# Gates of a product-key expert layer as fp32r matmuls of 256 columns, stored in contiguous blocks

## What is computed

```python
s1, i1 = lax.top_k(s[:, :, 0], PEER_TOPK)
s2, i2 = lax.top_k(s[:, :, 1], PEER_TOPK)
...
sc, pos = lax.top_k(cand, PEER_TOPK)
eidx = jnp.take_along_axis(cidx, pos, axis=-1)
gate = jax.nn.softmax(sc, axis=-1)
act = jax.nn.gelu(jnp.einsum('thkd,td->thk', e_u[eidx], xt).astype(jnp.float32))
w = (gate * act).astype(xt.dtype)
return jnp.einsum('thk,thkd->td', w, e_v[eidx])
```

## Time and profile before

| what | value |
|---|---|
| median of 3 runs | 4709.73 us (4707.64 to 4710.36) |
| profiled execution, its own time | 4707.14 us |
| its span in the trace | 4705.4 us |
| PE busy | 4426.2 us, 94% of the span |
| DVE / ACT / POOL busy | 2150.1 / 979.1 / 768.2 us |
| mean granted TensorE clock | 0.958 |
| chain that ended last | PE 87%, DMA 7%, DVE 2%, ACT 2% |

### The profile page before, as it was taken

How to read it: one execution, slowest core, us unless ns; L and a number is a source line. 1 busy time by engine, 2 the same in 40 slices (tenths; PEclk the granted TensorE clock), 3 DMA queues, 4 the chain that set the end, 5 groups by cost and what they waited for, 6 DMA issues and landing times.

```text
span 4705.4 us, 56888 instructions
## 1 busy us (share of the span) xinstructions
PE 4426.2 (94%) x23446; PEld 3833.8 (81%) x23446; DVE 2150.1 (46%) x3919; ACT 979.1 (21%) x1607; POOL 768.2 (16%) x532
## 2 busy tenths in 40 slices
PE   6898878879999999999999999979999999999999
PEld 4565546669999999999999999968878788787887
DVE  2222212121397667344444444435555555555554
ACT  1212111121122222222222222211111111111111
POOL 0000000011121222444444444400000000000000
PEclk8988779769999999999999999989999999999999
DMA  4000120011122222244443444464343433434332
GB/s 167 0 0 0 48 125 22 14 38 37 51 92 86 93 93 88 88 128 137 137 127 121 136 137 137 121 221 133 133 135 130 139 131 134 134 131 139 131 134 80
DMA packets 397825, 485.55 MB, mean 103 GB/s; under 512 B 290656, under 2 KB 308584, under 8 KB 396456
## 3 DMA queue, kind: packets, MB, share of 16 engines
q1 hardware_dynamic: 397624, 482.73, 31.2%
HBM read 329.78 MB, written 153.89 MB: 103 GB/s over the span
## 4 chain that ended last, share of the span: by engine, by line
PE 87%; DMA 7%; DVE 2%; ACT 2%; issue 1%; POOL 1%; DVEq 0%; ACTq 0%; SPq 0%; POOLq 0%
PE ps L311 77%; DMA ur<-u_t 5%; PE ps L1000 4%; PE ps L354 1%; PE ps L976 1%; PE ps L814 1%; PE ps L776 1%; DMA win<-w_in 0%; PE ps L305 0%; ACT uh L1045 0%; PE ps L819 0%; DMA gate_in<-gates 0%; DVE xT L552 0%; DMA vc_s<-vc 0%; PE ps L390 0%
## 5 line engine op out<-in xcount | busy, mean ns | idle before, releaser
L311 PE MATMUL ps<-xh,uh 128*128 128x364 f32 (+1 forms) x3456 | 1159.6, 336 | 24.3 <-issue 10.4
L311 PE MATMUL ps<-xh,ul 128*128 128x364 f32 (+1 forms) x3456 | 1140.5, 330 | 8.0 <-issue 8.0
L311 PE MATMUL ps<-xl,uh 128*128 128x364 f32 (+1 forms) x3456 | 1139.7, 330 | 0.0
L311 PE MATMUL ps<-vh,wh 128*128 128x512 f32 (+1 forms) x2304 | 898.2, 390 | 29.3 <-DVE wl L1257 29.3
L311 PE MATMUL ps<-vh,wl 128*128 128x512 f32 (+1 forms) x2304 | 898.1, 390 | 0.0
L311 PE MATMUL ps<-vl,wh 128*128 128x512 f32 (+1 forms) x2304 | 896.9, 389 | 0.0
L1266 DVE TENSOR_TENSOR acc<-acc,ps 128x512 f32<-128x512 f32 (+1 forms) x576 | 394.0, 685 | 710.6 <-PE ps L311 710.6
L311 PEld LDWEIGHTS ps<-xh,uh 128*128 128x128 f32 x3456 | 653.9, 189 | 29.1 <-issue 26.6
L311 PEld LDWEIGHTS ps<-xh,ul 128*128 128x128 f32 x3456 | 653.3, 189 | 10.0 <-issue 10.0
L311 PEld LDWEIGHTS ps<-xl,uh 128*128 128x128 f32 x3456 | 654.3, 189 | 0.0
L1089 POOL TENSOR_TENSOR ul<-ur,uh 128x1024 fp32r<-128x1024 f32 x144 | 362.7, 2519 | 1143.8 <-ACT uh L1045 1143.8
(11 more groups left out here) (210 smaller groups left out, 3567.4 us busy)
## 6 DMA issues: line engine op xcount, KB each, us to landing
hidden_after_gelu<-hid SPq DMA_DIRECT2D x128, 544.0 KB, 3.0
gates<-gs SPq DMA_DIRECT2D x17, 4096.0 KB, 21.1
act_in<-hidden_after_gelu SPq DMA_DIRECT2D x128, 544.0 KB, 5.7
gate_in<-gates SPq DMA_DIRECT2D x128, 544.0 KB, 6.6
ur<-u_t SPq DMA_DIRECT2D x128, 512.0 KB, 4.5
vr<-v_w SPq DMA_DIRECT2D x128, 512.0 KB, 3.5
ur<-wq SPq DMA_DIRECT2D x16, 512.0 KB, 4.1
win<-w_in SPq DMA_DIRECT2D x1, 7168.0 KB, 22.5
```

Of the source, the lines that this page charges most:

```text
L311: i = nc.tensor.matmul(out, lhsT, rhs, start=(k == 0), stop=(k == len(pairs) - 1))
```

## The change

1. Gate matmuls in fp32r. oneA holds plain ones and zeros (fp32r). oneB is `[128, 2, 4, 2, 128]`: for each token two halves side by side, the column one-hot times the high part of the gate (gh) and times the low part (gate minus gh). One matmul of 256 columns per token makes both halves; a quad fills two PSUM banks.
2. DVE makes oneB with 8 `tensor_scalar` per quad (is_equal with a per-partition scalar, times another one), in place of one instruction, and oneA as before. POOL's product is gone; POOL only does `split_low`.
3. ACT copies the high halves (`gates_high`) ahead of the gelu of the same group, and DVE adds the low halves to them (`gates_low`). `c_free` now comes from DVE.
4. PSUM: 4 banks for hidden groups (`h_bank`), 4 for quads. A quad stands behind every 18th matmul of a block, inside the groups.
5. The store of the gates goes out from ACT's queue, as contiguous 32 KB per partition; `gate_in` is now read in 17 pieces of 256 B per partition.
6. PICK = 5: GATE0 = 63, GATE1 = 131, so 13 hidden blocks follow the last gate. The transposes of a tile move behind the next tile's blocks, the last two tiles' come together; then ACT makes gh for all tokens, and DVE its low part.

```diff
-PICK = 6
+PICK = 5
-    gates_d = nc.dram_tensor("gates", [PK, PK, T], F32).ap()
+    gates_d = nc.dram_tensor("gates", [QUADS // HALF, 128, PK, 4 * HALF], F32).ap()
-    oneA = sb("oneA", [128, 4, 4, 128])
-    oneB = sb("oneB", [128, 4, 4, 128])
+    oneA = sb("oneA", [128, 4, 4, 128], F32R)
+    oneB = sb("oneB", [128, 2, 4, 2, 128], F32R)
...
+    def h_bank(g, k):
+
+        return (g * NG + k) % 4
...
-            need(e, "gelu", (g - 2) * NG + k + 1)
+            need(e, "gelu", g * NG + k - 3)
...
+                if quads is not None and (k * len(parts) + m) % 18 == 17:
+                    q = (k * len(parts) + m) // 18
+                    gate_quad(e, quads + q, q)
...
         e.wait_ge(sem("c_oneB"), n + 1)
-        e.wait_ge(sem("c_gated"), n + 1)
...
-            i = nc.tensor.matmul(ps[:, 6 + q % 2, k * 128:(k + 1) * 128], oneA[:, q, k, :], oneB[:, q, k, :],
-                                 start=True, stop=True)
+            i = nc.tensor.matmul(ps[:, 4 + 2 * (q % 2) + k // 2, (k % 2) * 256:(k % 2) * 256 + 256], oneA[:, q, k, :],
+                                 oneB[:, q % 2, k, :, :].rearrange("p a b -> p (a b)"), start=True, stop=True)
...
+        def picking(t, like):
             for j in range(PICK):
...
+            if like >= 1:
+                picks_transposed(e, t - 1, (like - 1) % 2)
...
+                if GATE0 <= g < GATE1:
+                    gates_high(e, (g - GATE0) * 4 + k)
...
+                if k == 0 and GATE0 + 4 <= g <= GATE1 and (g - GATE0) % 4 == 0:
+                    gates_out(e, (g - GATE0) // 4 - 1)
             if g + 2 < NB:
                 split_high(e, g + 2)
+            if GATE0 <= g < GATE1:
+                gates_high(e, (g - GATE0) * 4 + 3)
...
+            if t == NT and j == PICK - 1:
+                picks_kept(e, NT)
+                nc.scalar.activation(gh[:], selT[:, 2, :], ACT.Copy).then_inc(sem("gh_ready"), 1)
...
+        def operands(n):
+            need(e, "c_g", n - 3)
+            nc.vector.tensor_tensor(oneA[:, n % 4, :, :], iota.unsqueeze(1).to_broadcast([128, 4, 128]),
+                                    wide(selT[:, 0, 4 * n:4 * n + 4], 128), ALU.is_equal).then_inc(sem("c_oneA"), 1)
+            need(e, "c_g", n - 1)
+            for k in range(4):
+                tok = slice(4 * n + k, 4 * n + k + 1)
+                nc.vector.tensor_scalar(oneB[:, n % 2, k, 0, :], iota, selT[:, 1, tok], gh[:, tok].bitcast(F32),
+                                        ALU.is_equal, ALU.mult)
+                i = nc.vector.tensor_scalar(oneB[:, n % 2, k, 1, :], iota, selT[:, 1, tok], selT[:, 2, tok],
+                                            ALU.is_equal, ALU.mult)
+            i.then_inc(sem("c_oneB"), 1)
+
+        def gates_low(n):
+            e.wait_ge(sem("c_ghi"), n + 1)
+            nc.vector.tensor_tensor(kept(n), kept(n), quad_gates(n, 1), ALU.add).then_inc(sem("c_free"), 1)
+
+        operands(0)
+        operands(1)
         for n in range(QUADS):
+            gates_low(n)
+            if n + 2 < QUADS:
+                operands(n + 2)
...
-                load(gate_in[:, b % 2, :], gates_d[:, b, :], f"gate_in_{b % 2}")
+                load(gate_in[:, b % 2, :].rearrange("p (h t) -> p h t", t=4 * HALF), gates_d[:, :, b, :].rearrange("h p t -> p h t"), f"gate_in_{b % 2}")
```

More of the change, by code:

```diff
@@ L949, in x_pe, with hidden_block @@
             pe_transposes(xnc[:, n % 2, :], banks(2 * (n % 2), 2), width(n), "c_tx")
-    def hidden_block(e, g, par, after=None):
+    def h_bank(g, k):
+        return (g * NG + k) % 4
+    def hidden_block(e, g, like, quads=None):
+        par = like % 2
         e.wait_ge(sem("u_hi"), g + 1)
@@ L959, in hidden_block @@
         for k, (o, w) in enumerate(TG):
-            need(e, "gelu", (g - 2) * NG + k + 1)
+            need(e, "gelu", g * NG + k - 3)
             parts = [(a[:, par, dc * 128:(dc + 1) * 128], b[:, dc, o:o + w])
                      for dc in range(DC) for a, b in ((uh, xh), (uh, xl), (ul, xh))]
-            mm_sum(ps[:, 3 * par + k, 0:w], parts, "hidden")
-            if after:
-                after(k)
+            for m, (lhsT, rhs) in enumerate(parts):
+                i = nc.tensor.matmul(ps[:, h_bank(like, k), 0:w], lhsT, rhs, start=(m == 0), stop=(m == len(parts) - 1))
+                if m == len(parts) - 1:
+                    i.then_inc(sem("hidden"), 1)
+                if quads is not None and (k * len(parts) + m) % 18 == 17:
+                    q = (k * len(parts) + m) // 18
+                    gate_quad(e, quads + q, q)
     def key_scores(e, c):
@@ L1045, in split_high, with quad_gates, kept, gates_high @@
         nc.scalar.activation(uh[:, g % 2, :], ur[:, g % 2, :], ACT.Copy).then_inc(sem("u_hi"), 1)
-    def gates_kept(e, n):
+    def quad_gates(n, part):
+        return ps[:, 4 + 2 * (n % 2):6 + 2 * (n % 2), :].rearrange("p b (t s j) -> p s j (b t)", t=2, s=2)[:, part, :, :]
+    def kept(n):
+        s = n % HALF * 4
+        return gs[:, n // HALF % 2, :, s:s + 4]
+    def gates_high(e, n):
         hf = n // HALF
@@ L1080, in h_act @@
                 nc.scalar.activation(sel[0:p, t % 2, 2, :], sel[0:p, t % 2, 2, :], ACT.Exp).then_inc(sem("c_exp"), 1)
[L1081 to L1085, removed]
+            if 1 <= t <= NT and j == PICK - 1:
+                picks_kept(e, t - 1)
+            if t == NT and j == PICK - 1:
+                picks_kept(e, NT)
+                nc.scalar.activation(gh[:], selT[:, 2, :], ACT.Copy).then_inc(sem("gh_ready"), 1)
     def split_low(e, g):
@@ L1091, in h_pool @@
     def h_pool(e):
-        def weighted(n):
-            if n % 32 == 0:
-                e.wait_ge(sem("c_selT"), n // 32 + 1)
-            e.wait_ge(sem("c_oneA"), n + 1)
-            nc.gpsimd.tensor_tensor(oneA[:, n % 4, :, :], oneA[:, n % 4, :, :], wide(selT[:, 2, 4 * n:4 * n + 4], 128),
-                                    ALU.mult).then_inc(sem("c_gated"), 1)
-        for g in range(GATE0 + 1):
-            split_low(e, g)
-        for g in range(GATE0, GATE1):
-            n = (g - GATE0) * 4
-            weighted(n)
-            weighted(n + 1)
-            split_low(e, g + 1)
-            weighted(n + 2)
-            weighted(n + 3)
-        for g in range(GATE1 + 1, NB):
+        for g in range(NB):
             split_low(e, g)
@@ L1182, in h_dve @@
         softmaxed(e, ch, NT)
[L1184 to L1192 removed]
+        e.wait_ge(sem("c_selT"), NT + 1)
+        e.wait_ge(sem("gh_ready"), 1)
+        ch(nc.vector.tensor_tensor(selT[:, 2, :], selT[:, 2, :], gh[:].bitcast(F32), ALU.subtract))
+        iota = cst[:, C_IOTA:C_IOTA + 128]
+        def operands(n):
[3 more added lines that the diff above has]
+            need(e, "c_g", n - 1)
+            for k in range(4):
+                tok = slice(4 * n + k, 4 * n + k + 1)
[9 more added lines that the diff above has]
+        operands(1)
+        for n in range(QUADS):
+            gates_low(n)
+            if n + 2 < QUADS:
+                operands(n + 2)
     def output_quad(e, qd, par):
```

77 lines of the change are left out of this document (31 added, 46 removed).

## The result

| | before | after |
|---|---|---|
| median | 4708.68 us (4705.12 to 4710.36, 4 runs) | 4799.85 us (4798.37 to 4805.55, 4 runs) |
| profiled execution, span | 4707.14, 4705.4 | 4798.37, 4796.6 |
| granted clock | 0.958 | 0.944 |

Ratio 1.0197, 95% interval 1.0179 to 1.0215: slower by 2%, 91 us. The forecast was 4772, the range 4600 to 4840.

The account below looks back on a forecast made before the run. PE was taken to bound the gating stretch. Stall-lengthened blocks +49, clock +11, start of gates +5, behind gates -5.7 and gate_in loads +5 sum to +64 on 4707.1: forecast 4772 us, range 4600 to 4840.

Parts of the forecast that it names:

- clock: Gating stretch: PE's new stall halves the clock in one block in ten, +11 us, bounds 0 and 109.
- start of the gates: Before the first quad: last two tiles' transposes together, then gate copies, low part and first operands, together +5 us.
- behind the gates: The 4 blocks after the last gate lose a late weight load, 53.7 to 48.0, -5.7 us.
- gap: Ahead of the first output: four gate_in loads in 256 B pieces take longer, +5 us (0 to 10).
- the clock falls in most blocks: Gating stretch: the longer stall lowers the clock in most blocks, +98 on the forecast, 4870 us; chance 0.08.
- The loop's end: Gating stretch: a loop's end (1.9 us) falls into the stall before quad 0 and costs nothing.
- first rival: Gating stretch: POOL doesn't stop tensor_scalar, block 14.78 us, plus eight loop ends at 1.9; total 4616 us, chance 0.24.
- fourth rival: Gating stretch: stores still delay weight loads, 44 us on top of the forecast, 4816 us; chance 0.06.
- not stopped: Gating stretch: DVE's tensor_scalar runs on beside POOL's ul, stall 0.83 us, total 4616 us; chance 0.24.
- POOL waits for a pause: Gating stretch: POOL's ul starts only when DVE pauses, block 16.3 us, total 4704, no change; chance 0.13.
- float32's pace: Gate matmuls: 256 fp32r columns take 0.445 us, block 21.0, +312 us, total near 5020; chance 0.05.
- the stores still hold up the weights: Gating stretch: gate stores keep delaying weight loads as before, 44 us on top, 4816 us; chance 0.06.

Follow-up runs that it names:

- e2: Changed kernel with POOL making only half of ul's columns in the gating stage, the other half left stale: 4661.26 us.
- e3: Changed kernel with DVE making operands of quad n+2 ahead of the sum of quad n: 4605.29 us, ratio 0.9774 to the kernel before.
- e4: Changed kernel, order kept, with DVE instead of POOL making ul in the gating stage, behind each block's third quad's operands: 4653.73 us.
- e5: Changed kernel with DVE's operands ahead of its sums and ul made by DVE in the gating stage: 4554.54 us, ratio 0.9654 to the kernel before.
- e1: Changed kernel with twelve unused matmuls on PE ahead of the wait for quad 0's operands, once per block: 4776.58 us.
- e11: Kernel before with only the new stores (contiguous blocks from ACT's queue, gate_in in pieces): 4686.82 us, ratio 0.9938.
- e6: Changed kernel with picking in blocks of 6 again, 4 blocks behind the last gate: 4814.41 us, ratio 1.0196 to the kernel before.
- e7: Changed kernel with the old gate stores (256-byte strips from SP's queue, gate_in in one piece a partition): 4932.70 us, ratio 1.0454 to the kernel before.

## Why the prediction came out as it did

The mechanism was right: POOL's ul stops a tensor_scalar, the chain through ACT's copy, DVE's sum and the operands is longer than what PE has to do, and PE stands once a block ahead of the first quad. e2 shows it by a stop of half the length, e3 and e4 by taking either link out. The forecast lies 28 us under the measured 4800. By its terms:

| term | forecast | measured |
|---|---|---|
| a quad on PE | 0.49 | 0.47 |
| one tensor_scalar, pace | 0.256 | 0.26 |
| stop by POOL | 2.35 | 2.05 |
| chain ahead of quad 0 | 6.67 | 6.09 |
| stall | 3.18 | 2.62 |
| block, full clock | 17.13 | 16.78 |
| blocks, in the sum | +49 | 68 x (16.78 - 16.41) = +25 |
| clock | +11 | +66 |
| start of the gates | +5 | what these two leave of the stretch's 94.9: +3 |
| behind the gates | -5.7 | 53.7 to 4 x 11.98: -5.8; 9 moved blocks 108.7 to 107.8: -0.9 |
| gap | +5 | +3.3 |

With -0.8 ahead of the picking and +0.4 in the output the measured column adds to 91, the difference of the spans. The start of the gates has two waits of PE, 1.7 at the transposes and 2.7 ahead of the first quad. The 108.7 are nine of the 54 picking blocks that took 652.5 us before.

**The weakest step is the clock**, "one block in ten: +11". It was mis-sized, not missed: the bounds of that term were 0 and 109. A fall costs 2.0 us (66.5 over 33) where 1.6 was taken, and it comes in 33 of 67 blocks. The reason I gave, that the stage before stayed at 0.99 in spite of 43 us of gaps, compared the wrong thing: those gaps were few and far apart, the new ones are one in each block. The rival "the clock falls in most blocks" was the nearer one for this term. That the total came so near is in part luck, as two errors partly cancelled: the block was 0.35 us too dear (-24), the clock 55 too cheap. The block was too dear by its chain, 6.67 against 6.09, of which the stop is 0.3.

**The loop's end.** The number (nothing) was right, the reason is not enough: in e3 and e5 there is no stall into which 1.9 us could fall, and their distances show no pass's end either (14.87 to 14.94 in e3). It shows in e1, in e11 and in the kernel before, whose blocks have 100, 104 and 104 matmuls, and not in the kernels with 88. A pass of eight blocks is then 1600, 1664 and 1408 instructions, with a weight load for each matmul. The picking stage has a loop too, with passes of 12 blocks before and 20 in the change (1,728 and 2,880 such instructions), and there PE has a gap of 0.8 to 1.4 us ahead of the first matmul behind each jump back, in these kernels and in those without a gap in the gating stage. In e6, whose passes are 24 blocks, it moved with the jump from block 43 to block 48. So the gaps belong to the jump back, and the short passes have none. The Trainium skill (Runtime: NRT & Kernel Launch, Instruction fetch mechanics) says that PE's instruction memory holds 2048 instructions, refilled in blocks, and that a taken branch to a page outside the current window waits for a fetch. No run here shows that memory, and by the number alone passes of 1600 would still fit in; e1 changed the length of a pass together with PE's stall. The cause of the gaps stays open. (The first rival counted eight such ends; the loop jumps back six times.)

**Stores.** "0 here" was right for the time, since the prediction compared with the whole stage. But the prices given for them, 44 us in the kernel before and the same in the fourth rival, were wrong on both sides: without them the stage before gets only 16 us shorter (1111 to 1095 from first to last gate, e11), as 41 us of the loop's ends take their place, and under the new order they would have cost 133 (e7). Nor is 21.1 us what the weight load stood for, as the prediction has it: that is the landing of the store, and the load was held for 18.6 to 19.2. The change needed its new queue far more than the kernel before did.

**13 blocks behind the last gate, picking in 5:** nothing, as forecast (e6). **256 columns in fp32r** run near the pace worked out (0.122), at 0.118 us each. The rivals "not stopped" and "POOL waits for a pause" are excluded by the timeline, "float32's pace" by the 0.47 of a quad, and "the stores still hold up the weights" by there being no wait of ACT for ur in the stage.

## What to carry to other kernels

When work moves from one engine to another, write down the order in which the receiving engine now does things and follow one item round the loop: here the gain of 1.6 us a block on PE was lost because DVE added old gates before it made new operands, and two exchanged lines turned +2.0% into -2.3%. Ask which engine can stop the one that gets the work: POOL's ul cost 2 us a block until DVE did it in 1.2 itself. A small stall that recurs in every block can cost over a third as much again in clock (66 us beside 180 of stall), and removing one wait may uncover another that had hidden in it, so price both with the cover gone.

## What the runs showed that I had not expected

- A stall of 2.62 us once per 16.8 us took the clock down in half of the blocks and cost 66 us; one of 1.6 us once per 15.7 us (e2) never did. PE was busy with the same work in between.
- A weight load issued behind a store of 16,384 pieces of 256 bytes on the same queue held SP's sequencer for 18.7 us; behind the same 4 MB in contiguous blocks for 0.43; and strips from ACT's queue held up neither ACT's own instructions (the issue took 0.52) nor SP's sequencer (its longest issue of a load was 1.1). The loads beside them took 8.2 us to land instead of 4.3, which nothing waited for.
- The ends of the loop's passes cost 6.9 us each in e11 and 7.6 in e1, of which PE's two gaps are 4.1 and 4.8 (mean of six), with the lower clock behind them, and nothing in the gating stage of kernels with 88 matmuls a block.
